# Two weight slabs split ahead of the first MLP, one group of means, and a final norm in token layout, in a two-block transformer kernel

## The reference

```
block 1: h = rmsnorm(x) ; proj = h @ w_in
         x = x + rmsnorm((sig(g_a)*pool_mixer + sig(g_b)*conformer_conv) @ w_o, norm_mix_post)
         h = rmsnorm(x, norm_mlp_pre)
         x = x + rmsnorm(square(relu(h @ w_up)) @ w_down, norm_mlp_post)
block 2: attention (NSA) and gated linear attention side by side, x = x + merged @ w_out
         x = x + (silu(h @ w_gate) * (h @ w_up)) @ w_down
return rmsnorm(x, norm_final)        # x * rsqrt(mean(x*x) + 1e-6) * gain
```

## Time and profile before

| | us |
|---|---|
| median of 3 runs (1579.47 to 1580.46) | 1579.6 |
| the profiled execution's own time | 1579.75 |
| its span, first to last instruction | 1577.8 |
| TensorE busy | 1490.5 (94%) |
| VectorE busy | 788.6 (50%) |
| ScalarE busy | 505.8 (32%) |
| GpSimd busy | 156.2 (10%) |
| mean granted TensorE clock, share of full | 0.978 |

### The profile page before, as it was taken

How to read it: one execution, slowest core, us unless ns; L and a number is a source line. 1 busy time by engine, 2 the same in 40 slices (tenths; PEclk the granted TensorE clock), 3 DMA queues, 4 the chain that set the end, 5 groups by cost and what they waited for, 6 DMA issues and landing times.

```text
span 1577.8 us, 16902 instructions
## 1 busy us (share of the span) xinstructions
PE 1490.5 (94%) x7062; PEld 1202.7 (76%) x7062; DVE 788.6 (50%) x1011; ACT 505.8 (32%) x668; POOL 156.2 (10%) x114
## 2 busy tenths in 40 slices
PE   4999989799999999879989899999998999999997
PEld 3888768578888888648777587777886888888885
DVE  5999663544234343463683745455435433433433
ACT  4222343443332322244443333332233222212212
POOL 0040013000000000200240211110220000000001
PEclk9999999899999999989999999999998999999998
DMA  5332213122233232412331021010222323233221
GB/s 150 107 107 95 80 66 107 54 81 94 93 107 97 91 107 81 147 60 81 81 80 56 27 65 44 3 51 10 84 94 80 95 93 107 80 107 107 81 80 54
DMA packets 138136, 129.52 MB, mean 82 GB/s; under 512 B 14581, under 2 KB 134636, under 8 KB 138060
## 3 DMA queue, kind: packets, MB, share of 16 engines
q1 hardware_dynamic: 135552, 124.27, 25.2%
q0 software_dynamic: 992, 3.47, 0.7%
q10 hardware_dynamic: 1516, 0.69, 0.2%
HBM read 126.32 MB, written 2.10 MB: 81 GB/s over the span
## 4 chain that ended last, share of the span: by engine, by line
PE 88%; DVE 7%; ACT 2%; issue 2%; DMA 1%; POOL 0%; ACTq 0%; DVEq 0%; POOLq 0%
PE gemm L402 68%; PE gemm L773 4%; PE gemm L511 2%; PE misc L800 2%; PE misc L785 2%; PE gemm L428 1%; PE misc L793 1%; PE gemm L543 1%; PE misc L786 1%; DVE rstd L1306 1%; DMA conv_rows<-in_conv_w 1%; DVE w_lo L1297 1%; DVE q_level L1623 1%; PE misc L628 1%; ACT w_hi L879 1%
## 5 line engine op out<-in xcount | busy, mean ns | idle before, releaser
L402 PE MATMUL gemm<-h_hi,w_hi 128*128 128x512 f32 x1136 | 446.4, 393 | 5.2 <-DVE w_lo L1297 5.2
L402 PE MATMUL gemm<-h_lo,w_hi 128*128 128x512 f32 x1136 | 443.3, 390 | 0.0
L402 PE MATMUL gemm<-h_hi,w_lo 128*128 128x512 f32 x1136 | 443.2, 390 | 0.0
L1297 DVE TENSOR_TENSOR w_lo<-w_raw,w_hi 128x2048 fp32r<-128x2048 f32 (+1 forms) x111 | 251.4, 2265 | 190.7 <-ACT w_hi L879 190.6
L879 ACT ACTIVATE w_hi<-w_raw 128x2048 fp32r<-128x2048 f32 (+1 forms) x115 | 216.8, 1885 | 145.8 <-PE gemm L402 138.1
L402 PEld LDWEIGHTS gemm<-h_hi,w_hi 128*128 128x128 f32 x1136 | 214.2, 189 | 54.5 <-DVE w_lo L1297 6.3
L402 PEld LDWEIGHTS gemm<-h_hi,w_lo 128*128 128x128 f32 x1136 | 214.0, 188 | 44.6
L402 PEld LDWEIGHTS gemm<-h_lo,w_hi 128*128 128x128 f32 x1136 | 214.0, 188 | 44.6 <-issue 0.5
L402 PE MATMUL gemm<-f_hi,w_hi 128*128 128x512 f32 x432 | 168.0, 389 | 0.0
L402 PE MATMUL gemm<-f_lo,w_hi 128*128 128x512 f32 x432 | 168.0, 389 | 0.0
L402 PE MATMUL gemm<-f_hi,w_lo 128*128 128x512 f32 x432 | 168.0, 389 | 0.0
(11 more groups left out here) (329 smaller groups left out, 1658.8 us busy)
## 6 DMA issues: line engine op xcount, KB each, us to landing
w_raw<-in_w_in SPq DMA_DIRECT2D x62, 512.0 KB, 4.6
w_raw<-in_w_down SPq DMA_DIRECT2D x32, 512.0 KB, 4.1
w_raw<-in_w_up SPq DMA_DIRECT2D x30, 512.0 KB, 4.6
w_raw<-in_w_ffn_gate SPq DMA_DIRECT2D x22, 512.0 KB, 4.4
w_raw<-in_w_ffn_up SPq DMA_DIRECT2D x22, 512.0 KB, 4.7
w_raw<-in_w_ffn_down SPq DMA_DIRECT2D x16, 512.0 KB, 4.0
w_raw<-in_w_o SPq DMA_DIRECT2D x8, 512.0 KB, 4.5
w_raw<-in_w_out SPq DMA_DIRECT2D x8, 512.0 KB, 4.1
```

The costliest lines, as they stand in the source:

```text
L402: mm = nc.tensor.matmul(bank[:], w[s % RING][:, kt, col0:col0 + P], x(n), start=first, stop=last)
L1297: V.tensor_tensor(part(lo_of(s), s), part(raw_of(s), s), f(part(hi_of(s), s)), SUB).then_inc(S("lo_done"), 1)
```

## The change

It has three parts. (1) Slabs 23 and 24 (`EARLY`) both get buffers of their own, with the lo written over the raw data; their loads wait only for the end of the phase before "wo", count on semaphores of their own, and their hi splits don't wait for the product of slab s-2. ScalarE splits both in step k = 6 of "wo", right behind slab 22; VectorE makes both lo parts behind that of slab 22. (2) In `first_up` the means of squares of all eight tiles come in one group behind the last hi matmuls, and `spread_rstd` between the first and the second block's products with `HLO`. (3) In "fdown2" ScalarE also writes XT * gain (`XG`) for tiles 0 to 6, VectorE for tile 7; the mean is taken with the squares as weights and one column of 1/1024, so that it comes out as one number per token, tokens on the partitions; the tiles are transposed before the factor is known, partly between the two halves of the mean, into seven different PSUM banks; root and reciprocal are of 128 x 4 elements, and the evacuation to `OTK` multiplies by the factor of the token: five tiles on VectorE, three on ScalarE in four instructions each.

```diff
-    UPRAW, UPHI, UPLO = at("up_raw", [KT, SLAB], f32, R1 + 32), at("up_hi", ..., R1 + 40), at("up_lo", ..., R1 + 48)
+    UPRAW = [at(f"up_raw{i}", [KT, SLAB], f32, R1 + 32 + 16 * i) for i in range(2)]
+    UPLO = [at(f"up_lo{i}", [KT, SLAB], f32r, R1 + 32 + 16 * i) for i in range(2)]
+    UPHI = [at(f"up_hi{i}", [KT, SLAB], f32r, R1 + 40 + 16 * i) for i in range(2)]
     def raw_full(s):
-        return raw_ready[s % RING], 16 * sum(PIECES[s % RING:s + 1:RING])
+        if s in EARLY:
+            return S(f"up_raw_ready{EARLY[s]}"), 32
+        return raw_ready[s % RING], 16 * sum(PIECES[x] for x in range(s % RING, s + 1, RING) if x not in EARLY)
-    SECOND_UP = PH["up0"][0] + 1
+    EARLY = {PH["up0"][0] + 1: 0, PH["up0"][0] + 2: 1}
...
+    XG = at("x_gained", [KT, T], f32, 16)
+    OUT_BANKS = M[0:3] + [G[(PH["fdown2"][2] + k) % 4] for k in (7, 4, 5, 6)] + M[0:1]
+    DVE_TILES, ACT_TILES = (0, 2, 4, 6, 7), (1, 3, 5)
     def load(s, pieces):                                    # SP
+            if s in EARLY:
+                sp.wait_ge(S("block_full"), PH["wo"][2])
+                for dst, src in pieces:
+                    sp.dma_start(dst, src).then_inc(S(f"up_raw_ready{EARLY[s]}"), 16)
+                return
             if s >= RING:
                 sp.wait_ge(S("lo_done"), s - 1)
-            if s == SECOND_UP:
-                sp.wait_ge(S("block_full"), PH["wo"][2])
         for k in range(KT):                                 # SP, the stores
-            sp.wait_ge(S("out_ready"), k + 1)
+            if k in DVE_TILES:
+                sp.wait_ge(S("out_ready"), DVE_TILES.index(k) + 1)
+            else:
+                sp.wait_ge(S("odd_out_ready"), ACT_TILES.index(k) + 1)
     def first_up():                                         # TensorE
-                for e in {0: (), 6: (5, 6, 7), 7: ()}.get(k, (k - 1,)):
-                    pe.wait_ge(S("x1_squared"), e + 1)
-                    mm = mean_rows(Y[:, e, :], e == 0, e == KT - 1)
-                    if e == KT - 1:
-                        mm.then_inc(S("mean_ready"), 1)
-            spread_rstd(M[2], 2)
+            for k in range(KT):
+                pe.wait_ge(S("x1_squared"), k + 1)
+                mm = mean_rows(Y[:, k, :], k == 0, k == KT - 1)
+            mm.then_inc(S("mean_ready"), 1)
             for b in range(4):
+                if b == 1:
+                    spread_rstd(M[2], 2)
...
-        mean_of_sum(3, (S("ysq_ready"), 3 * KT))            # TensorE, the end
-        for k in range(KT):
-            pe.wait_ge(S("hs_ready"), 3 * KT + k + 1)
-            if k >= 4:
-                pe.wait_ge(S("out_ready"), k - 3)
-            bank = M[k % 4]
-            for t in range(TT):
-                mm = nc.tensor.transpose(bank[...], HS[k % 2][:, t * P:(t + 1) * P], IDENT[:])
-            mm.then_inc(S("out_T"), 1)
+        def out_tile(k):
+            pe.wait_ge(S("x_gained"), k + 1)
+            for t in range(TT):
+                mm = nc.tensor.transpose(OUT_BANKS[k][...], XG[:, k, t * P:(t + 1) * P], IDENT[:])
+            mm.then_inc(S("out_T"), 1)
+        pe.wait_ge(S("sq_added"), 4 * KT)
+        for t in range(TT):
+            nc.tensor.matmul(M[3][:, t:t + 1], SQA[:, t * P:(t + 1) * P], INV[1024][:, 0:1], start=t == 0, stop=False)
+        out_tile(0)
+        out_tile(1)
+        pe.wait_ge(S("ysq_ready"), 3 * KT)
+        for t in range(TT):
+            mm = nc.tensor.matmul(M[3][:, t:t + 1], SQ[1][:, t * P:(t + 1) * P], INV[1024][:, 0:1], start=False, stop=t == TT - 1)
+        mm.then_inc(S("mean_ready"), 1)
+        out_tile(2)
+        pe.wait_ge(*evac_at(b0 + KT - 1))
+        for k in range(3, 7):
+            out_tile(k)
+        pe.wait_ge(S("out_ready"), 1)
+        out_tile(7)
     def split_hi(s):                                        # ScalarE
-                if s >= RING:
+                if s >= RING and s not in EARLY:
                     act.wait_ge(S("block_full"), BLOCKS_BEFORE[s - 1])
             if k % 2 == 0:                                  # ScalarE, step k of "wo"
                 split_hi(s0 + k // 2 + 1)
+            if k == KT - 2:
+                split_hi(s0 + 5)
+                split_hi(s0 + 6)
             if k == KT - 1:
-                split_hi(SECOND_UP)
                 nc.scalar.activation(TMP16[:, 0:1], EPSB[:], ACT.Sqrt)
...
         for k in range(KT):                                 # ScalarE, "fdown2"
+            if k % 2 == 0:
+                split_hi(s0 + k // 2 + 1)
+            if k == KT - 1:
+                A_(TMP16[:, 0:1], EPSB[:], ACT.Sqrt)
+            last(k, b0 + k, 0)
+            if k < KT - 1:
+                A_(XG[:, k, :], XT[:, k, :], ACT.Copy, scale=col("norm_final_2", k)).then_inc(S("x_gained"), 1)
+        act.wait_ge(S("mean_ready"), 7)
+        A_(ROOT_TOK[:], M[3][:, 0:TT], ACT.Sqrt, bias=EPSB[:]).then_inc(S("out_rooted"), 1)
+        act.wait_ge(S("out_inverted"), 1)
+        for k in ACT_TILES:
+            act.wait_ge(S("out_T"), k + 1)
+            for t in range(TT):
+                ins = A_(OTK[:, t, k * P:(k + 1) * P], OUT_BANKS[k][...], ACT.Copy, scale=RSTD_TOK[:, t:t + 1])
+            ins.then_inc(S("odd_out_ready"), 1)
         run("wo", nothing)                                  # VectorE
-        split_lo(SECOND_UP)
+        for s in EARLY:
+            split_lo(s)
...
-        invert(6, (S("hs_ready"), 3 * KT))                  # VectorE, the end
-        for k in range(KT):
-            if k >= 2:
-                dve.wait_ge(S("out_T"), k - 1)
-            V.scalar_tensor_tensor(HS[k % 2][:], XT[:, k, :], col("norm_final_2", k), RSTD[:], MUL, MUL)...
+        dve.wait_ge(*evac_at(b0 + KT - 1))
+        dve.wait_ge(S("x_gained"), KT - 1)
+        V.tensor_scalar(XG[:, KT - 1, :], XT[:, KT - 1, :], col("norm_final_2", KT - 1), None, MUL)...
+        dve.wait_ge(S("out_rooted"), 1)
+        V.reciprocal(RSTD_TOK[:], ROOT_TOK[:]).then_inc(S("out_inverted"), 1)
+        dve.wait_ge(S("out_inverted"), 1)
+        for k in DVE_TILES:
+            dve.wait_ge(S("out_T"), k + 1)
+            V.tensor_tensor(OTK[:, :, k * P:(k + 1) * P], OUT_BANKS[k][:].rearrange("p (t d) -> p t d", d=P),
+                            RSTD_TOK[:].unsqueeze(2).broadcast_to([P, TT, P]), MUL).then_inc(S("out_ready"), 1)
```

More of the change, by code:

```diff
@@ L161, in build @@
     PHI, PLO = at("pool_hi", [POOL_G, T], f32r, R1 + 48.5), at("pool_lo", [POOL_G, T], f32r, R1 + 56.5)
-    UPRAW, UPHI, UPLO = at("up_raw", [KT, SLAB], f32, R1 + 32), at("up_hi", [KT, SLAB], f32r, R1 + 40), at("up_lo", [KT, SLAB], f32r, R1 + 48)
+    UPRAW = [at(f"up_raw{i}", [KT, SLAB], f32, R1 + 32 + 16 * i) for i in range(2)]
+    UPLO = [at(f"up_lo{i}", [KT, SLAB], f32r, R1 + 32 + 16 * i) for i in range(2)]
+    UPHI = [at(f"up_hi{i}", [KT, SLAB], f32r, R1 + 40 + 16 * i) for i in range(2)]
     CHI, CLO = at("conv_hi", [CC, T], f32r, R1 + 64.5), at("conv_lo", [CC, T], f32r, R1 + 72.5)
@@ L215, in evac_at @@
         return evac[m % 4], m // 4 + 2 + i * (per // 4)
-    SECOND_UP = PH["up0"][0] + 1
+    EARLY = {PH["up0"][0] + 1: 0, PH["up0"][0] + 2: 1}
     def raw_of(s):
-        return UPRAW if s == SECOND_UP else RAW[s % RING]
+        return UPRAW[EARLY[s]] if s in EARLY else RAW[s % RING]
     def hi_of(s):
-        return UPHI if s == SECOND_UP else WHI[s % RING]
+        return UPHI[EARLY[s]] if s in EARLY else WHI[s % RING]
     def lo_of(s):
-        return UPLO if s == SECOND_UP else WLO[s % RING]
+        return UPLO[EARLY[s]] if s in EARLY else WLO[s % RING]
     def part(t, s):
@@ L291, in build @@
     OTK = at("out_tokens", [TT, D], f32, R1)
+    XG = at("x_gained", [KT, T], f32, 16)
+    ROOT_TOK, RSTD_TOK = at("out_root", [TT], f32, SB + 12), at("out_rstd", [TT], f32, SB + 12.5)
+    OUT_BANKS = M[0:3] + [G[(PH["fdown2"][2] + k) % 4] for k in (7, 4, 5, 6)] + M[0:1]
     read = [S(f"misc_read{i}") for i in range(4)]
+    DVE_TILES, ACT_TILES = (0, 2, 4, 6, 7), (1, 3, 5)
     H2, F2 = 7 * KT, 4 * KT
@@ L399, in gemm @@
                     ready(n)
-                for w, x in ((WHI, hi), (WHI, lo), (WLO, hi)):
-                    last = n == len(kts) - 1 and w is WLO
-                    mm = nc.tensor.matmul(bank[:], w[s % RING][:, kt, col0:col0 + P], x(n), start=first, stop=last)
+                for w, x in ((hi_of, hi), (hi_of, lo), (lo_of, hi)):
+                    last = n == len(kts) - 1 and w is lo_of
+                    mm = nc.tensor.matmul(bank[:], w(s)[:, kt, col0:col0 + P], x(n), start=first, stop=last)
                     first = False
@@ L847, in _ @@
         run("fdown2", h(FHI[0]), h(FLO[0]), kts=range(6), ready=h_ready(fbase + 2 * KT))
-        mean_of_sum(3, (S("ysq_ready"), 3 * KT))
-        for k in range(KT):
-            pe.wait_ge(S("hs_ready"), 3 * KT + k + 1)
-            if k >= 4:
-                pe.wait_ge(S("out_ready"), k - 3)
-            bank = M[k % 4]
+        def out_tile(k):
+            pe.wait_ge(S("x_gained"), k + 1)
             for t in range(TT):
```

(23 more changed lines are left out.)

2 lines of the change are left out of this document (1 added, 1 removed).

## The result

The changed kernel takes **1565.94 us** (median of 4 runs, 1564.5 to 1566.11), the kernel before beside it 1580.03 us (1579.47 to 1581.62): a ratio of 0.9907, 95% interval 0.989 to 0.9924. The forecast was 1564.0 with a range of 1560.5 to 1567.5, so the sign and the range held and the middle was 1.9 us low. The profiled execution took 1566.09 us (span 1564.1), 13.66 us less than the profiled 1579.75 of before. One execution of an experiment further down (y2_pairs, 2511 us at a granted clock of 0.554) was in the chip's slower state and is left out everywhere.

The account below looks back on a forecast made before the run. TensorE, 88% of the chain of waits, was taken to bound the kernel; 10.4 us early plus 5.2 at the end, 15.6 off the profiled 1579.75, gave 1564.15, as median 1564.0 us, range 1560.5 to 1567.5.

Parts of the forecast that it names:

- The wait for the last square: Before the means of "wo": with early hi splits and table load, the mean starts at 286.85 instead of 290.18, gaining 3.35 us.
- The spread: Before first_up: the spread comes earlier, while the clock is still full; between 0 and 1.0 us, taken as 1.0.
- The means in one group: In first_up: six groups of means of squares become one, saving 5 x 0.32 = 1.6 us.
- The stall before slab 24: TensorE's 3.25 us wait before slab 24 goes, with 1.2 us of slow matmuls behind it; together 4.45 us.
- Slab 25: Next to be late, 2.4 us to spare; rival that it becomes the new wait: 1568.4 us, 7%.
- The first store: At the end: without the table load and with a small root and reciprocal, the first store comes 4.9 us earlier.
- The store: At the end: eight stores at 287 GB/s take 7.3 us instead of 7.6, gaining 0.3 us.
- The rival of stores at the load's rate: At the end: stores are bound by how tiles come and run at the load's rate; 1562.2 us, 5%.
- The ScalarE queue at k = 6: In "wo": late raw data for slab 24's hi delay the last square; slower, up to 1583.5 us at 301; 3%.
- the clock case: Rival: the clock doesn't fall before first_up; 1.9 us more gain, 1562.1 us, 12%.
- the lower price of the means: At the end: SQA's four mean matmuls cost 0.43 us instead of the 0.9 taken.
- the end rival: The end hangs on the tiles after all, so half of the 5.2 us stays; 1566.6 us, 5%.

Follow-up runs that it names:

- y2_pairs: The changed kernel with its output stored in four transfers of two tiles each instead of eight of one; 1565.8 us.
- z1_wait23: The changed kernel with slab 24 back in the ring and slab 23's hi part back behind the last product of w_o; 1576.63 us.
- x2_means: The changed kernel with the means of squares in first_up put back between the hi matmuls, the spread right behind them; 1571.22 us.
- x4_slab24: The changed kernel with slab 24 back in the ring, split behind the evacuation of the first two blocks; slab 23 stays early; 1570.85 us.
- z2_slack: The changed kernel with two more unread subtractions on VectorE directly before its lo part of slab 25; 1568.53 us.
- y3_half: The changed kernel storing only the first four of the eight output tiles, all arithmetic kept; 1562.63 us.
- y5_best: The changed kernel with unread matmuls in two gaps (16 before first_up, 25 before the last feed-forward part) and stores of 1, 2, 2 and 3 tiles; 1560.48 us.
- y1_fill: The changed kernel with thirteen unread matmuls on TensorE between the group of means of squares and the first up matmuls; 1564.99 us.
- x3_tail: The changed kernel with only the old end put back: feature layout, 128 x 512 root and reciprocal, transposes after the factor; 1570.53 us.
- y4_fillall: The changed kernel with thirteen unread matmuls before first_up and 24 in each gap before the gated-attention block and last feed-forward part; 1562.54 us.

## Why the prediction was right, point by point

- **The wait for the last square**, 3.35 predicted: 3.70 to 0.28, 3.42 us. **The spread**, 1.0: 2.07 to 1.16, 0.91. Both return in z1_wait23. ScalarE's room was put at 1.5 us and was 1.89.
- **The means in one group**, 1.6: 1.73 by x2_means, the place of the spread with it. The group of eight tiles took 1.89 us in the chain, 0.24 per tile.
- **The stall before slab 24**, 4.45: together with the three terms above I had 10.4; the trace has 9.14 + 1.2 = 10.3. x4_slab24 gives 3.90 for the idle time alone. The spell of half clock before it stayed, as I took, but two more matmuls fell into it, 0.4 us that I had put at nothing.
- **Slab 25**, 2.4 us to spare: 2.0 by the trace (331.14 against 333.12), 2.1 by z2_slack. The rival was right about what is next in line and had no cause to act.
- **The first store**, 4.9 earlier: 5.6. The terms that I had sized too high: `SQA`'s means 0.79 for 0.9; two tiles' transposes 0.93 for 1.3, because I took a row of four alone (0.67), and a row's length holds some 0.2 us at its end that the next group covers (4 records 0.64, 8 records 1.07, 16 records 1.91); the last means 0.80 for 0.9; the reciprocal 0.19 for 0.3. ScalarE's tile copies were 0.27 to 0.29 each, not 0.37, so the tiles came early enough. **The store**, 0.3: 0.55.
- **The rival of stores at the load's rate** had its mechanism right as to who binds (y3_half) and wrong as to the rate; y2_pairs and y5_best show that longer runs, not earlier tiles, would bring it.
- **The ScalarE queue at k = 6**: the two early hi parts ran back to back from 280.08, so their data were there. It never came near deciding.
- **The range** doesn't follow from the parts that I named: the clock case with the lower price of the means is 1562.1 - 0.9 = 1561.2, not 1560.5, and the end rival with a spell twice as long 1566.6 + 1.9 = 1568.5, not 1567.5. The measured time lies inside either pair.
- **The step that missed** was the assumption in the sum that the rest of the kernel takes its old time. The changed places gave 16.5 us, 0.9 more than the sum; the identical ones took 2.8 more in the profiled pair. Shown is that it goes with spells of half clock falling elsewhere. Between slab 24 and the last product the same work took 1228.9 us with 34.1 us at half clock (the changed kernel, twice), 1229.8 with 37.5 (y2_pairs, y3_half), 1230.9 with 41.0 (y1_fill) and 1231.5 with 44.4 (x2_means), so each us at half clock costs about a quarter of one there. x2_means, x4_slab24 and z1_wait23 cost 0.8 to 3.3 us more in the median than locally, x3_tail 1.3 less. Shown too is that the first 2.07 us are no cost of the change: the code up to `SQA`'s mean is the same in the changed kernel and in eight of the experiments with an edit, and reaches it between 285.6 us (y1_fill, 7.0 us at half clock behind the first product) and 288.6 (x3_tail, 12.2), the kernel before at 286.05. But of that one there is a single trace, and all of the eight but y1_fill lie above it. Not shown is what decides where the spells outside the long waits fall. That the forecast of the whole came within 1.9 us is in part luck: 0.9 us more gain and 2.8 us of loss partly cancelled.

## What to carry to other kernels

Where one engine is 88% of the chain, read its idle times and the clock behind each, and count a wait as its length plus the slow instructions after it, unless something else is already waited for there. Check what local gains are worth on stretches between fixed points of the same engine; the whole time scatters by as much as such a term (1.6 us over four runs of the changed kernel, 3.8 over five of x3_tail). At a kernel's end, ask for the length of the contiguous runs before asking for earlier tiles.

## What the runs showed of the hardware that I had not expected

- Matmuls whose result nobody reads held the granted clock at 1.00 over a gap behind which it had been 0.50, at no cost to the real ones: 18 records, nine matmuls, in 2.17 us, and `SQA`'s mean to slab 24 2.5 us shorter.
- At a DMA share of 1.01 the stores ran at 288 GB/s with runs of 512 B, 341 with 1 KB and 369 with 1.5 KB.
- The length of an idle time alone doesn't tell whether half clock follows. One of 2.32 us (z2_slack) was followed by full clock, one of 2.94 by half at once, one of 3.76 (x4_slab24) by half 1.3 us later, and in the changed kernel one of only 1.70 us by half within 0.9 us:

```profile
685.20 0.50 PE L416 MATMUL gemm<-h_hi,w_hi 128*128 128x512 f32 x1 [1.70 <-DVE w_lo L1335]
...
686.10 0.63 PE L416 MATMUL gemm<-h_hi,w_hi 128*128 128x512 f32 x1
```

- A granted clock of 1.00 isn't yet the full pace: the 16 hi matmuls behind the second filled gap (y4_fillall) came every 0.33 us, as ScalarE's tiles came (0.66 us for two matmuls), where the same form came every 0.23 behind the third.
